# Pooling mixer begun with the attention mixer, a norm's spread four steps later, one weight split ahead of each norm

## The chip, the core and the metric

The kernel runs on one core of a Trainium2 chip. The metric is device time in microseconds of one execution. The core has four engines that compute, each with its own instruction stream, run in order: TensorE (PE) multiplies, VectorE (DVE), ScalarE (ACT) and GpSimd (POOL) do the elementwise work. SyncE (SP) issues the transfers from memory. Engines wait for each other by semaphores alone.

## The reference

Two transformer blocks over 256 tokens of width 1024, all in float32. What the change touches lies in the first block:

```python
def rmsnorm(x, w):
    return x * rsqrt(mean(x * x, -1) + EPS) * w

def pool_mixer(u, w_pool, scale):          # u: 256 tokens, 4 groups of 128 channels
    # trailing mean over 2, 4, 8, 16 tokens (one window a group) minus u itself,
    # then one 128x128 product a group, times scale
    p = stack([(c - lag) / cnt - u_g for each group])
    return einsum('btgc,gcd->btgd', p, w_pool).reshape(B, T, 512) * scale

def first_block(x, ...):
    proj = rmsnorm(x, norm_mix_pre) @ w_in
    gq, gk, gv, gg1, gr, pu, mq, mk, mv, gates = split(proj)
    ya = gla_mixer(gq, gk, gv, gg1, gr, ...) @ w_branch_a
    yb = pool_mixer(pu, pool_w, pool_scale) @ w_branch_b
    yc = moba_mixer(mq, mk, mv) @ w_branch_c       # here plain causal attention, 8 heads
    gs = sigmoid(gates)
    mixed = gs[0] * ya + gs[1] * yb + gs[2] * yc
    x = x + rmsnorm(mixed @ w_out, norm_mix_post)
    f = (silu(h @ w_gate) * (h @ w_up)) @ w_down   # h = rmsnorm(x, norm_ffn_pre)
    return x + rmsnorm(f, norm_ffn_post)
```

The second block has a feed-forward part, two attention mixers, a cross attention to a second input `mem`, and another feed-forward part. Keys and values of that memory are `rmsnorm(mem, mem_kv_norm) @ mem_w_kv`; their four products (`mkv0` to `mkv3`) are computed early, in the first block's time.

## The kernel before

**Units.** All weights lie in one flat array, cut into 360 units of 128x1024 numbers (512 KB) or less. SP fetches a unit into one of four buffers `raw`. ACT rounds it to an upper part `whi` (L1279), DVE subtracts to get the lower part `wlo` (L1627); together this is "the split of unit u". PE then multiplies three times: upper by upper, lower by upper, upper by lower (L806 to L808 where the weights are stationary or stream 512 columns, L814 to L817 where features stream 256). A unit is 12 matmuls of 512 columns or 24 of 256. The split of u needs the slot of u-4, so it waits until PE has multiplied u-4, and SP fetches u+4 once DVE has split u.

**The order.** One function, `order`, writes a list of steps, and every engine walks through this same list and issues its own share of each step. The order of each engine's instructions is fixed by it. The steps are: `split u`, `unit u`, `end name` (a finished product is taken out of PSUM), `do name`, and `step name`, one slice of a task that runs beside the products. `spawn` starts a task, `tick` gives each running task one step after each unit, in the order in which the tasks were spawned. A unit's splits stand `AHEAD = 2` units before it. Engines drift apart as far as the semaphores let them.

**The tasks the change touches.** `pool` has five steps. POOL adds the shifted sequences (L2263 to L2273, then the means at the margin, L2278), DVE forms mean minus input (L1879, tile `m_pp`) in step 2, PE multiplies with the group weights (L923) in step 5, ACT scales and rounds the result into `m_br_hi` (L1290 and L1291), DVE into `m_br_lo` (L1638), both in step 5. It is spawned after product `pu` (units 13 to 16), so its steps follow units 17 to 21 and run beside the task `gla` (25 steps, after units 9 to 33), whose masked copies out of PSUM are L1852 on DVE and whose score matmuls are L881 on PE. `moba` (15 steps) is spawned when `gla` is over, after product `gt1`, so its steps follow units 37 to 51: scores (L984) in step 4, row maxima (L1901) and their negation (L1907) on DVE, the exponential (L1403) on ACT in step 5, the transposes of its result (L961) on PE in step 6.

`memory` (12 steps, after units 53 to 64) loads, transposes and squares the second input; its root of the mean square is computed by POOL and DVE, and in the last step `across(4)` spreads it over the partitions: DVE writes two diagonals (L1672), PE multiplies them with ones (L848), DVE copies the result out (L1675). It is used first at the end of `mkv0`.

**Around each norm.** Products `wo0` and `wo1` (units 65 to 72, woven) and `f0dn0`, `f0dn1` (units up to 142) each end in `out_rms`: ACT squares (L1300), DVE scales (L1737). Then `sum_of` forms the root (L1743, POOL's power L2231, L1650 to L1656) and adds to x (L1750, four instructions). PE multiplies two units of the memory's keys in that time (73 and 74, and 143 and 144), then transposes half of the new x (L834), multiplies unit 75 (or 145), transposes the other half, and goes on.

PSUM has eight banks in two rings of four: big ones for the products of weights, small ones for all else. A small bank is taken again four takes later, and its next writer waits until the last reader is through.

Of the kernel before, what the change touches and what calls it, by code (L numbers as in the profile page):

```python
# [23 lines left out]
AHEAD = 2  # L24
# [261 lines left out]
for _n in range(11):  # L286
    for _name, _of in (("f0", "n1"), ("f1", "n2"), ("f2", "n6")):
        PRODUCTS[f"{_name}gu{_n}"] = ("b", _of)
NORMS = ("norm_mix_pre", "norm_ffn_pre", "ffn1_norm_2", "mix_norm_2", "mem_kv_norm_2", "mem_q_norm_2", "ffn2_norm_2")

STEPS = {"gla": 25, "pool": 5, "moba": 15, "fox": 13, "cmp": 9, "sel": 8, "win": 8, "mixed_first": 1, "mixed_second": 1, "yc": 1, "onsa": 1, "ofox": 1, "rel": 8, "memory": 12, "w1": 17,
         "gf_tokens": 2, "y_first": 1, "y_second": 1, **{f"mem{h}": 4 for h in range(4)}, "end_first": 2}
# [13 lines left out]
def order(chunks, n_units):  # L306
# [9 lines left out]
    def tick():  # L316
        for name in list(left):
            yield "step", name, 0, 0
            left[name] -= 1
            if not left[name]:  # L320
                del left[name]
                for n in THEN.get(name, ()):
                    spawn(n)
# [6 lines left out]
    def spawn(name):  # L330
        left[name] = STEPS[name]

    def do(name):
        yield "do", name, 0, 0

    def product(name, mid={}, end_first=False):
        for j, u in enumerate(chunks[name]):
            yield from split_to(u + AHEAD)
            if j in mid:
                yield from mid[j]()  # L340
            yield "unit", name, j, u
            if end_first and u == chunks[name][-1]:
                yield "end", name, 0, 0
            yield from tick()
        if not end_first:
            yield "end", name, 0, 0
# [11 lines left out]

    def woven(halves, mid={}, then={}):

        n = len(chunks[halves[0]]) // 2
        for i, (name, j) in enumerate((name, j) for first in (0, n) for name in halves for j in range(first, first + n)):
            u = chunks[name][j]
            yield from split_to(u + AHEAD)
            if i in mid:
                yield from mid[i]()
            yield "unit", name, j, u
            yield from tick()
            if j == 2 * n - 1:
                yield "end", name, 0, 0  # L370
                if name in then:
                    spawn(then[name])
# [10 lines left out]
    spawn("gla")  # L383
    for name in ("gr", "pu"):
        yield from product(name)
    spawn("pool")
    for name in ("mq", "mk", "mv"):
        yield from product(name)
    moba = False
    for n in range(6):  # L390
        yield from product(f"gt{n}")
        if not moba and "gla" not in left:
            spawn("moba")
            moba = True
    yield from drain()
    if not moba:
        spawn("moba")
        yield from drain()
    spawn("memory")
    for n in range(2):  # L400
        for i in range(3):
            yield from product(f"br{i}{n}")
        spawn(("mixed_first", "mixed_second")[n])
    yield from woven(("wo0", "wo1"))
    yield from drain()
# [5 lines left out]
    yield from product("f0dn0", {10: drain})  # L411
    yield from product("f0dn1")
    yield from do("sum1")
# [51 lines left out]
def build(nc, io):  # L465
    with ExitStack() as ctx:
# [248 lines left out]
        def gaps(i):  # L715
            return 2 if i == 5 else 3

# [553 lines left out]
        def scalar(q):  # L1271
# [228 lines left out]
            def memory():  # L1500
                for _ in range(6):
                    yield
                for n in range(2):
                    half(4, n)
                    squares(4, n)
                    yield
                for _ in range(3):
                    yield
# [792 lines left out]
        def sync(q):  # L2301
# [70 lines left out]
            def memory():  # L2372
                q.wait_ge(*ps.out("moba", "values", 1))
                load("mem", memx[:, :, :], io["mem_2"].rearrange("a (k p) d -> p (a k) d", p=128))
                for _ in range(11):
                    yield
# [111 lines left out]
```

## Time and profile before

| | |
|---|---|
| median of 3 runs | 1180.5 us (1178.74 to 1180.65) |
| the profiled execution | 1182.92 us, its span 1180.8 us |
| PE busy | 1136.7 us, 96% |
| DVE busy | 707.1 us, 60% |
| ACT busy | 562.4 us, 48% |
| POOL busy | 22.1 us, 2% |
| granted PE clock, mean | 0.986 of full |
| read from memory | 204.74 MB, 178 GB/s over the span |

All times in this document that have a place ("at 87.79") are microseconds from the span's start in the profiled execution. The profiled execution has 2.1 us around its span. A row of a timeline gives the start, the duration, the engine and the source line, then the tile that is written and those that are read, and in brackets how long the engine had been idle and what ended that. Neighbouring instructions of one kind are merged into one row, with their number behind the x. What PE is doing can be read only roughly from its busy share, since matmuls overlap; where its next start is late, it stood still.

### The profile page before, as it was taken

Reading aid. Unit: us, or ns where it says so; the run is one execution under the profiler, and the core shown is the slowest. Engines: PE = TensorE matmul, PEld = TensorE weight load, DVE = VectorE, ACT = ScalarE, POOL = GpSimd, SP = SyncE. Lnnn points to the kernel's source line nnn. Section 1 sums busy time; section 2 is a strip of 40 time slices with the busy share of each in tenths; the row PEclk is TensorE's granted clock in tenths of the full one; section 3 lists DMA queues with packets and bytes.
Section 4 is the critical chain, followed back from the end, with each engine's and each line's share of the span. In section 5 each row is a group of like instructions: output and inputs, shape, how many; then the busy total and the mean of one; then the engine's idle time right before and its main releaser. Section 6 shows DMA issues by size and latency. Waiting matters only on the chain.

```text
span 1180.8 us, 18370 instructions
## 1 busy us (share of the span) xinstructions
PE 1136.7 (96%) x7638; PEld 1021.9 (87%) x7638; DVE 707.1 (60%) x1069; ACT 562.4 (48%) x844; POOL 22.1 (2%) x43
## 2 busy tenths in 40 slices
PE   6989999999999999999999998999999999999996
PEld 6878878879999988899998897687888898999985
DVE  4676544867666646566665553355657556666653
ACT  5534556545444444544544436145654545544442
POOL 0030000000000000000000000000000000000000
PEclk9999999999999999999999998999999999999998
DMA  7544453554665764576656587222336335556561
GB/s 261 179 133 136 160 212 125 199 174 156 207 191 191 229 195 159 179 265 198 194 185 205 193 278 262 72 90 90 124 126 249 128 109 186 188 190 202 190 208 65
DMA packets 62653, 209.08 MB, mean 177 GB/s; under 512 B 7307, under 2 KB 14523, under 8 KB 61804
## 3 DMA queue, kind: packets, MB, share of 16 engines
q1 hardware_dynamic: 61148, 206.07, 52.9%
q10 hardware_dynamic: 1424, 1.85, 0.4%
q8 instruction: 60, 0.98, 0.3%
q14 instruction: 21, 0.17, 0.0%
HBM read 204.74 MB, written 5.26 MB: 178 GB/s over the span
## 4 chain that ended last, share of the span: by engine, by line
PE 85%; DVE 7%; ACT 3%; DMA 2%; issue 2%; POOL 1%; ACTq 0%; DVEq 0%; POOLq 0%
PE ps L814 13%; PE ps L806 12%; PE ps L817 12%; PE ps L816 12%; PE ps L808 12%; PE ps L807 12%; DMA raw<-in_wflat 2%; DVE wlo_b L1627 2%; PE ps L1059 1%; PE ps L834 1%; PE ps L1011 1%; PE ps L973 1%; ACT m_Pb L1403 1%; DVE wlo L1627 1%; PE ps L1046 1%
## 5 line engine op out<-in xcount | busy, mean ns | idle before, releaser
L814 PE MATMUL ps<-hT_hi,whi_b 128*128 128x256 f32 x1392 | 389.0, 279 | 5.2 <-DVE wlo_b L1627 5.2
L816 PE MATMUL ps<-hT_hi,wlo_b 128*128 128x256 f32 x1392 | 385.9, 277 | 0.0
L817 PE MATMUL ps<-hT_lo,whi_b 128*128 128x256 f32 x1392 | 385.6, 277 | 0.0
L1627 DVE TENSOR_TENSOR wlo_b<-raw,whi_b 128x1024 fp32r<-128x1024 f32 x184 | 219.1, 1212 | 124.2 <-ACT whi_b L1279 124.0
L1627 DVE TENSOR_TENSOR wlo<-raw,whi 128x1024 fp32r<-128x1024 f32 x176 | 212.3, 1222 | 117.3 <-ACT whi L1279 116.4
L814 PEld LDWEIGHTS ps<-hT_hi,whi_b 128*128 128x128 f32 x1392 | 262.8, 189 | 7.7 <-issue 5.6
L816 PEld LDWEIGHTS ps<-hT_hi,wlo_b 128*128 128x128 f32 x1392 | 262.9, 189 | 0.4
L817 PEld LDWEIGHTS ps<-hT_lo,whi_b 128*128 128x128 f32 x1392 | 262.7, 189 | 0.0
L1279 ACT ACTIVATE whi<-raw 128x1024 fp32r<-128x1024 f32 x176 | 181.6, 1057 | 112.9 <-PE ps L808 86.7
L1279 ACT ACTIVATE whi_b<-raw 128x1024 fp32r<-128x1024 f32 x184 | 184.1, 1042 | 32.7 <-PE ps L808 13.6
L806 PE MATMUL ps<-whi,hT_hi 128*128 128x512 f32 (+1 forms) x272 | 110.0, 404 | 0.0
L807 PE MATMUL ps<-wlo,hT_hi 128*128 128x512 f32 (+1 forms) x272 | 106.5, 392 | 0.0
L808 PE MATMUL ps<-whi,hT_lo 128*128 128x512 f32 (+1 forms) x272 | 106.5, 392 | 0.0
L806 PE MATMUL ps<-whi,f_hid_hi 128*128 128x512 f32 x264 | 102.8, 390 | 0.0
L807 PE MATMUL ps<-wlo,f_hid_hi 128*128 128x512 f32 x264 | 102.7, 389 | 0.0
L808 PE MATMUL ps<-whi,f_hid_lo 128*128 128x512 f32 x264 | 102.7, 389 | 0.0
L1345 ACT ACTIVATE f_sg<-f_sg 128x512 f32<-128x512 f32 x33 | 20.9, 633 | 125.0 <-DVE f_sg L1769 125.0
L806 PEld LDWEIGHTS ps<-whi,hT_hi 128*128 128x128 f32 x272 | 53.0, 195 | 13.1 <-issue 1.8
L808 PEld LDWEIGHTS ps<-whi,hT_lo 128*128 128x128 f32 x272 | 52.6, 193 | 10.8
L807 PEld LDWEIGHTS ps<-wlo,hT_hi 128*128 128x128 f32 x272 | 52.8, 194 | 9.2
L808 PEld LDWEIGHTS ps<-whi,f_hid_lo 128*128 128x128 f32 x264 | 49.6, 188 | 10.3
L806 PEld LDWEIGHTS ps<-whi,f_hid_hi 128*128 128x128 f32 x264 | 49.6, 188 | 10.2
(313 smaller groups left out, 1283.1 us busy)
## 6 DMA issues: line engine op xcount, KB each, us to landing
raw<-in_wflat SPq DMA_DIRECT2D x358, 512.0 KB, 4.1
wide<-scratch SPq DMA_DIRECT2D x1, 2048.0 KB, 10.8
m_w<-in_cmp_k_w SPq DMA_DIRECT2D x4, 512.0 KB, 9.4
m_w<-in_cmp_v_w SPq DMA_DIRECT2D x4, 512.0 KB, 8.9
m_alibi<-in_c_alibi SPq DMA_DIRECT2D x1, 1536.0 KB, 7.4
x<-in_x SPq DMA_DIRECT2D x2, 512.0 KB, 4.7
m_memx<-in_mem SPq DMA_DIRECT2D x1, 1024.0 KB, 5.9
kept_ck<-m_ckT SPq DMA_DIRECT2D x1, 1024.0 KB, 7.9
```

Source lines behind the costliest of these rows:

```text
L806: e.matmul(o, xh, hi[:, k, :], start=first and k == 0, stop=False)
L807: e.matmul(o, xh, lo[:, k, :], start=False, stop=False)
L808: r = e.matmul(o, xl, hi[:, k, :], start=False, stop=last and k == kt - 1)
L814: e.matmul(o, hi[:, k, c], xs.h(k0 + k), start=first and k == 0 and f % 2 == 0, stop=False, skip_group_check=True)
L816: e.matmul(o, lo[:, k, c], xs.h(k0 + k), start=False, stop=False, skip_group_check=True)
L817: r = e.matmul(o, hi[:, k, c], xs.l(k0 + k), start=False, stop=last and k == kt - 1, skip_group_check=True)
L834: r = e.transpose(s[:, 256 * i + 128 * t:256 * i + 128 * t + 128], src(t)[:, 128 * (f + i):128 * (f + i) + 128], ident)
L973: r = e.matmul(s[:, 64 * h:64 * h + 64], PT[:, h * (qb + 1) + k, :], value(h, k), start=k == 0, stop=k == qb)
L1011: r = e.matmul(s[:, 64 * h:64 * h + 64], PTs[qb][:, h * (qb + 1) + k, :], value(h, k), start=k == 0, stop=k == qb)
L1279: e.activation(slot(whi, u)[:, 0:k * n], raw[u % NRAW][:, 0:k * n], ACT.Copy).then_inc(*w_hi.did(u))
L1345: e.activation(b, b, ACT.Silu).then_inc(*silu.did(i, c))
L1627: e.tensor_tensor(slot(wlo, u)[:, 0:k * n], r, h.bitcast(F32), ALU.subtract).then_inc(*w_lo.did(u))
```

## The change

Three things are altered, all in the list that `order` writes and in the numbers of steps.

- `pool` is spawned together with `moba`, just ahead of it, after `gt1`, and no longer after `pu`. Its five steps now follow units 37 to 41, and on every engine each stands ahead of moba's step after the same unit.
- `gaps(4)` is 7, no longer 3: the last step of `memory` with `across(4)` follows unit 68 (the second of `wo1`), no longer unit 64. The numbers of empty steps on ACT and SP follow suit.
- `woven` and `product` take an argument `ahead`. For `wo0`/`wo1` and for `f0dn1` it is 3: behind the last unit, and ahead of the `end` step, one more split is written, that of unit 75 and of unit 145. (Units 73, 74, 143 and 144 are split there already.)

```diff
-"memory": 12,
+"memory": 16,
@@ product, woven @@
+            if u == chunks[name][-1]:
+                yield from split_to(u + ahead)
@@ order @@
-    for name in ("gr", "pu"):
-        yield from product(name)
-    spawn("pool")
-    for name in ("mq", "mk", "mv"):
+    for name in ("gr", "pu", "mq", "mk", "mv"):
         yield from product(name)
     moba = False
     for n in range(6):
         yield from product(f"gt{n}")
         if not moba and "gla" not in left:
+            spawn("pool")
             spawn("moba")
             moba = True
     yield from drain()
-    if not moba:
-        spawn("moba")
-        yield from drain()
     spawn("memory")
...
-    yield from woven(("wo0", "wo1"))
+    yield from woven(("wo0", "wo1"), ahead=AHEAD + 1)
...
-    yield from product("f0dn1")
+    yield from product("f0dn1", ahead=AHEAD + 1)
...
         def gaps(i):
-            return 2 if i == 5 else 3
+            return {4: 7, 5: 2}.get(i, 3)
```

The changed kernel's line numbers are one lower than those before, from `order` on. In the rows that follow, `wlo_b_67`, `wlo_68` and so on are the buffers of the lower part, one of them to a unit.

First place, DVE beside the early part of `gla`. Before:

```order
L1627 TENSOR_TENSOR wlo_b_65<-raw_52,whi_b_57 128x1024
L1852 COPY_PREDICATED m_acc<-m_msk,ps 128x2x128 x4
L1879 SCALAR_TENSOR_TENSOR m_pp<-m_t_102,m_pu 128x256
...
L1627 TENSOR_TENSOR wlo_b_67<-raw_53,whi_b_59 128x1024
L1852 COPY_PREDICATED m_acc<-m_msk,ps 128x2x128 x4
L1627 TENSOR_TENSOR wlo_b_69<-raw_54,whi_b_61 128x1024
```

In the changed kernel, the same place:

```order
L1626 TENSOR_TENSOR wlo_b_65<-raw_52,whi_b_57 128x1024
L1851 COPY_PREDICATED m_acc<-m_msk,ps 128x2x128 x4
L1626 TENSOR_TENSOR wlo_b_67<-raw_53,whi_b_59 128x1024
L1851 COPY_PREDICATED m_acc<-m_msk,ps 128x2x128 x4
L1626 TENSOR_TENSOR wlo_b_69<-raw_54,whi_b_61 128x1024
```

The four instructions that write `m_pp` are gone from between the splits of units 20 and 21; on PE the four products L923 are likewise gone from behind unit 21.

Second place, ACT at the first exponential of `moba` (`whi_62` is unit 43's upper part, `m_Pb` holds the scores). Before:

```order
L1322 ACTIVATE m_gates<-ps,stat 128x512 x2
L1279 ACTIVATE whi_62<-raw_55 128x1024
L1403 ACT_TABLE_LOAD
L1403 ACTIVATE m_Pb,sm<-m_Pb,sm 128x128 x8
L1279 ACTIVATE whi_56<-raw_52 128x1024
```

In the changed kernel:

```order
L1321 ACTIVATE m_gates<-ps,stat 128x512 x2
L1278 ACTIVATE whi_62<-raw_55 128x1024
L1289 ACTIVATE m_br_hi<-ps,cols 128x256
L1290 ACTIVATE m_br_hi<-ps,cols 128x256
L1289 ACTIVATE m_br_hi<-ps,cols 128x256
L1290 ACTIVATE m_br_hi<-ps,cols 128x256
L1402 ACT_TABLE_LOAD
L1402 ACTIVATE m_Pb,sm<-m_Pb,sm 128x128 x8
```

The pooled result's four instructions, which wait for PE's L923 behind unit 41, now stand between unit 43's upper part and the exponential; on DVE the four of `m_br_lo` stand ahead of L1907 in the same way.

Third place, DVE at the end of the branch products (`diag` and `rT` are of `across(4)`). Before:

```order
L1627 TENSOR_TENSOR wlo_66<-raw_53,whi_58 128x1024
L1627 TENSOR_TENSOR wlo_68<-raw_54,whi_60 128x1024
L1672 TENSOR_SCALAR diag<-cst,stat 128x128 x2
L1675 COPY rT_81<-ps 128x256
L1729 TENSOR_TENSOR m_mtmp<-ps,m_gates 128x512
```

In the changed kernel:

```order
L1626 TENSOR_TENSOR wlo_66<-raw_53,whi_58 128x1024
L1626 TENSOR_TENSOR wlo_68<-raw_54,whi_60 128x1024
L1728 TENSOR_TENSOR m_mtmp<-ps,m_gates 128x512
L1730 TENSOR_TENSOR m_mixed<-m_mixed,m_mtmp 128x512
```

The splits of units 65 and 66 are now followed at once by the mixing; the diagonals stand four splits further on.

## Rows read from the trace of the kernel before

**Rows 1.** The page, the chain of waits that ended last, by engine.

```profile
PE 85%; DVE 7%; ACT 3%; DMA 2%; issue 2%; POOL 1%; ACTq 0%; DVEq 0%; POOLq 0%
```

**Rows 2.** Timeline of PE, 79 to 91 us (columns as told above).

```profile
80.75 0.36 PE L814 MATMUL ps<-hT_hi,whi_b 128*128 128x256 f32 x1 [1.24 <-DVE wlo_b L1627]
...
87.79 2.88 PE L923 MATMUL ps<-m_pp,m_wpl 128*128 128x256 f32 x8 [2.72 <-DVE m_acc L1852]
90.11 0.78 PE L814 MATMUL ps<-hT_hi,whi_b 128*128 128x256 f32 x1
```

**Rows 3.** Timeline of DVE, 60 to 92 us.

```profile
70.12 2.35 DVE L1627 TENSOR_TENSOR wlo_b<-raw,whi_b 128x1024 fp32r<-128x1024 f32 x2
...
77.95 1.50 DVE L1879 SCALAR_TENSOR_TENSOR m_pp<-m_t,m_pu 128x256 f32<-128x256 f32 x4 [4.11 <-POOL m_t L2273]
```

**Rows 4.** Timeline of POOL, 60 to 92 us.

```profile
70.64 3.69 POOL L2266 TENSOR_TENSOR m_t<-m_pu 128x1084 f32<-128x1084 f32 x1
74.41 1.53 POOL L2268 TENSOR_TENSOR m_t<-m_t 128x807 f32<-128x807 f32 x1
```

**Rows 5.** Busy time by stretch: PE, PEld, DVE, ACT, POOL; then clock, DMA.

```profile
88.80:92.10 3.30, 3.30 (x13) 2.94 (x12) 1.39 (x4) 2.23 (x5) 0.00 (x0) 0.50 0.17 70
239.00:242.20 3.20, 3.20 (x9) 2.49 (x8) 3.13 (x6) 0.00 (x0) 0.00 (x0) 0.50 0.54 189
462.00:467.00 5.00, 3.46 (x29) 3.05 (x28) 5.00 (x7) 2.67 (x6) 0.00 (x0) 1.00 0.00 1
```

**Rows 6.** Timeline of DVE, 446 to 454 us, where PE sets the pace.

```profile
448.17 1.23 DVE L1627 TENSOR_TENSOR wlo<-raw,whi 128x1024 fp32r<-128x1024 f32 x1 [1.49 <-ACT whi L1279]
450.89 1.23 DVE L1627 TENSOR_TENSOR wlo_b<-raw,whi_b 128x1024 fp32r<-128x1024 f32 x1 [1.50 <-ACT whi_b L1279]
```

**Rows 7.** Timelines of POOL and of DVE, 118 to 150 us.

```profile
125.73 1.01 POOL L2231 TENSOR_TENSOR sm<-sm,expo 128x4 f32<-128x4 f32 x1
...
129.27 1.22 DVE L1627 TENSOR_TENSOR wlo<-raw,whi 128x1024 fp32r<-128x1024 f32 x1
...
143.72 3.50 DVE L1627 TENSOR_TENSOR wlo<-raw,whi 128x1024 fp32r<-128x1024 f32 x3 [5.31 <-ACT whi L1279]
```

**Rows 8.** Timeline of ACT: the pooled result, the exponential, another table load.

```profile
89.01 0.47 ACT L1290 ACTIVATE m_br_hi<-ps,cols 128x256 fp32r<-128x256 f32 x1 [13.36 <-PE ps L923]
...
156.61 0.40 ACT L1403 ACTIVATE m_Pb<-m_Pb,sm 128x128 f32<-128x128 f32 x1 [0.74 <-DVE sm L1907]
...
183.82 1.28 ACT L1322 ACT_TABLE_LOAD   x1
185.12 1.27 ACT L1322 ACTIVATE m_gates<-ps,stat 128x512 f32<-128x512 f32 x2
```

**Rows 9.** Timeline of PE, 155 to 160 us.

```profile
155.97 0.39 PE L808 MATMUL ps<-whi,hT_lo 128*128 128x512 f32 x1
...
159.86 0.33 PE L961 MATMUL ps<-cst,m_Pb 128*128 128x128 f32 x1 [0.78 <-ACT m_Pb L1403]
```

**Rows 10.** Timelines of PE and of DVE, 235 to 244 us.

```profile
238.12 0.71 PE L848 MATMUL ps<-diag,ones 128*128 128x128 f32 x4 [2.30 <-DVE diag L1672]
...
243.01 1.03 PE L834 MATMUL ps<-cst,m_mixed 128*128 128x128 f32 x8
243.80 0.47 PE L806 MATMUL ps<-whi,hT_hi 128*128 128x512 f32 x1
...
235.32 2.35 DVE L1627 TENSOR_TENSOR wlo<-raw,whi 128x1024 fp32r<-128x1024 f32 x2
...
239.21 0.68 DVE L1729 TENSOR_TENSOR m_mtmp<-ps,m_gates 128x512 f32<-128x512 f32 x1
```

**Rows 11.** Timelines of PE at both norms, and of ACT at the first.

```profile
271.16 0.38 PE L814 MATMUL ps<-m_n_hi,whi_b 128*128 128x256 f32 x1 [1.35 <-DVE wlo_b L1627]
...
465.92 0.38 PE L814 MATMUL ps<-m_n_hi,whi_b 128*128 128x256 f32 x1 [1.31 <-DVE wlo_b L1627]
...
263.14 0.60 ACT L1300 ACTIVATE junk<-ps 128x512 f32<-128x512 f32 x1 [2.13 <-PE ps L808]
```

More of the change, by code:

```diff
@@ L289 @@
 NORMS = ("norm_mix_pre", "norm_ffn_pre", "ffn1_norm_2", "mix_norm_2", "mem_kv_norm_2", "mem_q_norm_2", "ffn2_norm_2")
-STEPS = {"gla": 25, "pool": 5, "moba": 15, "fox": 13, "cmp": 9, "sel": 8, "win": 8, "mixed_first": 1, "mixed_second": 1, "yc": 1, "onsa": 1, "ofox": 1, "rel": 8, "memory": 12, "w1": 17,
+STEPS = {"gla": 25, "pool": 5, "moba": 15, "fox": 13, "cmp": 9, "sel": 8, "win": 8, "mixed_first": 1, "mixed_second": 1, "yc": 1, "onsa": 1, "ofox": 1, "rel": 8, "memory": 16, "w1": 17,
          "gf_tokens": 2, "y_first": 1, "y_second": 1, **{f"mem{h}": 4 for h in range(4)}, "end_first": 2}
@@ L334, in do, with product @@
         yield "do", name, 0, 0
-    def product(name, mid={}, end_first=False):
+    def product(name, mid={}, end_first=False, ahead=0):
         for j, u in enumerate(chunks[name]):
@@ L357, in ffn, with woven @@
             spawn(f"turn{i}_{c}")
-    def woven(halves, mid={}, then={}):
+    def woven(halves, mid={}, then={}, ahead=0):
         n = len(chunks[halves[0]]) // 2
@@ L368, in woven @@
             yield from tick()
+            if u == chunks[halves[1]][-1]:
+                yield from split_to(u + ahead)
             if j == 2 * n - 1:
@@ L1506, in memory @@
                     yield
-                for _ in range(3):
+                for _ in range(gaps(4)):
                     yield
@@ L2374, in memory @@
                 load("mem", memx[:, :, :], io["mem_2"].rearrange("a (k p) d -> p (a k) d", p=128))
-                for _ in range(11):
+                for _ in range(15):
                     yield
```

## The prediction

> **What bounds the kernel now.** I read the chain of waits first. PE holds 85% of it, DVE 7%, ACT 3% [rows 1], so an edit is worth what it takes out of PE's standing still, and nothing else. Then I went through PE's timeline for late starts. They add up to some 30 us in the whole span; five of them stand where the change touches something. The rest of PE's time is units, one every 2.72 us: where PE alone sets the pace, DVE's splits start 450.89 - 448.17 = 2.72 us apart [rows 6].
>
> The first two are in the early part of `gla`. PE's unit 21 starts at 80.75 after 1.24 us idle, waiting for its lower part, and the pooling product L923 starts at 87.79 after 2.72 us idle, waiting for a small bank that DVE's masked copies free late [rows 2]. Both have one cause: at 77.95 DVE had stood 4.11 us for POOL's window sums [rows 3], with the split of unit 21 queued behind. The third is `across(4)`: 2.30 us idle before L848, waiting for DVE's diagonal [rows 10]. The last two are at the norms: 1.35 and 1.31 us before unit 75 and unit 145, waiting for a split that DVE does only after it has added to x [rows 11].
>
> The holes cost more than their length. After the one that ends at 87.79 the granted clock is 0.50, that is 1.2 instead of 2.4 GHz, from 88.8 to 92.1, and after the one that ends at 238.12 again from 239.0 to 242.2. After the hole of 1.31 us it stays 1.00 [rows 5].
>
> **The change part by part.** Places are given in the time of before, without the shift gained earlier.
>
> *Pooling leaves the early place.* DVE's four L1879 and the wait of 4.11 us go, so unit 21's split is done near 75.0 instead of 80.6. PE starts unit 21 when its score matmuls end: 1.2 us gained. Then nothing stands between the last score matmuls and unit 22: the hole of 2.7 us goes, and the product itself, which held PE from 87.79 to 90.11, 2.3 us [rows 2]. Of the half-clock stretch 90.11 to 92.1 is unit work, 2.0 us at half speed, so 1.0 us comes back; with the switching between kinds of matmul, 0.1 to 0.2 us, I take 1.2. Together 7.4 us. What is late next? Unit 22 would start near 83.8; DVE has split it by 78. The score matmuls after unit 25 come near 94.8; they need banks that the masked copies of the previous pair free near 84.6, and DVE's eight products before them are through near 90. Nothing else on SP or POOL is passed: SP's list is unchanged, and the two powers of POOL that pooling is moved past come forward. Bounds: at least the two waits' own 1.2 + 2.7 = 3.9, at most 7.7.
>
> *Pooling enters the late place.* POOL can begin once its second power is through, 125.73 + 1.0 = 126.7 [rows 7]. Its sums took from 70.64 to about 77.9, 7.3 us [rows 4, 3], so they end near 134. DVE wants them behind the split of unit 40, the second of the three at 143.72 [rows 7], so near 146: no wait, 12 us to spare. The 1.5 us of L1879 lie in DVE's slack (5.31 us idle ahead of that row).
>
> The product is another matter. PE does it after unit 41, whose last matmul starts at 155.97 [rows 9], so from 156.2. Eight passes over 256 columns, at the pace of the transposes (eight over 128 in 243.80 - 243.01 = 0.79 us [rows 10]), are 1.6 us; I take 1.7. ACT took up the pooled result 1.22 us after the product began (89.01 against 87.79 [rows 8, 2]), so now at 157.4. Four activations, 0.4 us apart, end at 159.0. Behind them in ACT's queue stands the table load for the exponential, 1.28 us [rows 8]; before, it lay in time in which ACT waited anyway. So the exponential starts at 160.3 instead of 156.61 [rows 8]: 3.7 us later. DVE's lower parts end near 159.9 and the negated maxima at 160.1, just hidden. PE's transposes L961 already waited for the exponential (0.78 us idle at 159.86 [rows 9]); they now start at 163.5. This term is -3.7 us, product included. Bounds: -1.7 (the product alone, everything else hidden) to -4.3 (the product as slow as before, 2.3 us).
>
> PE has only the product and unit 42 to fill the time: 156.2 + 1.7 + 2.7 = 160.6. It stands still for 2.9 us. Holes of this size in the same company were followed by the half clock twice [rows 2, 10, 5], so I expect a stretch of 3.4 us at half speed behind it, in unit work: -1.7 us. Bounds 0 to -1.8.
>
> By the Trainium skill, "ScalarE: Activation LUTs", section "What ACT_TABLE_LOAD costs", a switch costs a drain of about 1.38 us on top of the load. The trace does not show it: the load at 183.82 took 1.28 us and the next activation starts at 185.12 [rows 8]. With it, the term of the exponential would be -5.1 and the total 1.4 us smaller.
>
> *The spread four steps later.* Without the diagonals, PE goes from unit 64 (over at 235.7) to unit 65, which waits for DVE's split: the first of the two that start at 235.32 [rows 10], so to 236.5. Then unit 65 to 239.2, and the transposes of `mixed`, which need the four mixing instructions. DVE starts these at 237.6 instead of 239.21, at 0.66 us each (0.68 with overlap [rows 10]), so they end at 240.3. The transposes start there instead of at 243.01 [rows 10]: 2.7 us gained, in place of the 2.30 us hole two of 0.8 and 1.1 us. In it is 1.6 us for a half-clock stretch that falls away; if it stays, 1.1 is left. At its new place PE's L848 stands after unit 68, near 249; DVE's diagonal is written before that, near 247, and its user comes 25 us later. The copy that waits there for PE has the split of unit 71 behind it, done near 251.5 and needed at 255. Bounds +1.0 to +3.0.
>
> *One split ahead, twice.* ACT's part of unit 75 falls in the 2.13 us in which it waits for the last unit of `wo1` [rows 11], since it needs only unit 71. DVE's, 1.2 us, follows and ends 0.4 us before the squares release L1737. So nothing is pushed back, and the holes of 1.35 and 1.31 us at the two norms go: with the overlap of matmuls 1.45 each, 2.9. The next thing due, unit 76, is split within 1.2 us of x. Bounds 2.2 to 3.0.
>
> **The sum.** 7.4 - 3.7 - 1.7 + 2.7 + 2.9 = 7.6 us. Against the profiled execution's 1182.92 that gives 1175.3; it lay 2.4 above the median of the three runs, so for the median I say 1180.5 - 7.6 = 1172.9.
>
> **The rivals.**
>
> *No half clock at the exponential.* For it: the clock after the 1.31 us hole stayed full, so not every hole is followed by a slow stretch. Against it: 2.30 and 2.72 us idle both were. 1180.5 - 9.3 = 1171.2.
>
> *POOL and DVE hinder each other at the new place.* POOL's L2266 took 3.69 us for 1084 elements, 3.4 ns each, while DVE was in its two splits from 70.12; L2268, with DVE idle, took 1.53 us for 807, 1.9 ns each [rows 3, 4]. So POOL is slowed by DVE, and DVE was not slowed: 2.35 us for two splits is their usual length. At the new place POOL runs from 126.7 beside the splits of units 34 to 38, and if it were DVE that is held, for at most the 5.4 us that the four sums take alone, then PE's unit 34 at 133, whose split ended at 130.5 [rows 7], would be up to 2.9 us late. 1172.9 + 2.9 = 1175.8. The Trainium skill, "SBUF — State Buffer", section "SBUF: two separate sides", has one port pair for both engines, held by whichever starts first for its whole instruction; for POOL's lost time the trace agrees, for DVE's no row shows it.
>
> *The half clock also at the two small holes* of 0.8 and 1.1 us before the mixing: 1172.9 + 1.6 = 1174.5. Only the closeness of the two speaks for it.
>
> *The waits are handed on.* If DVE is the true bound at these places, each wait that goes is taken over by the next item in its queue, and every term lies at its lower bound: 3.9 - 4.3 - 1.7 + 1.0 + 2.2 = 1.1 us, so 1179.4, no measurable change. For it: DVE is busy for all of 462 to 467 [rows 5] and stands behind four of the five holes. Against it: the slack of several microseconds worked out above.
>
> *Slower: POOL late at the new place.* DVE waits in order at L1879 behind unit 40, with the splits of 41 and 42 behind it; each microsecond that POOL is later than 146 holds PE for one. POOL needs 7.3 us from 126.7, and at its slow rate of 3.4 ns an element throughout 9.2, ending at 136. It would decide from 146 on, and make the kernel slower only beyond 146 + 7.6 + 2.4, that is 156, four times as long; then 1183 or more.
>
> **How the numbers follow.** 0.50 for the forecast, 0.25 for no half clock at the exponential, 0.10 for the hindrance, 0.07 for the half clock at the small holes, 0.05 for no net gain, 0.03 for slower. Within 0.2% (2.4 us, about what can be told from no change) lies the fifth alone. So faster 0.92, same 0.05, slower 0.03. The range 1169.5 to 1176.5 takes in the first four with the runs' own spread of 1 us either side.
>
> **What would show it.** Right: no wait of DVE for POOL near 78; score matmuls of the second pair of heads about 7.5 us earlier; L848 with no idle time; units 75 and 145 straight behind the transposes; at L961 about 2.9 us idle for ACT, with the four L1290/L1291 and the table load just ahead of the exponential, and a clock of 0.50 behind it. Wrong: a new wait of PE between units 21 and 34, DVE waiting at L1879, or L1737 held by the early split.

## The result: 1175.5 us, half of the forecast gain

The changed kernel takes 1175.52 us, median of 20 runs (1170.95 to 1181.41), against 1180.51 for 20 runs of the kernel before. The ratio, run beside run, is 0.9968, with a 95% interval of 0.9953 to 0.9983: 3.8 us less, between 2.0 and 5.5. The medians lie 5.0 us apart, but the ratio compares runs taken side by side, and I go by it. The forecast was 7.6 us. Measured twice more, beside other runs of the kernel before, the ratio was 0.9965 and 0.9949.

The profiled execution lasted 1172.54 us with a span of 1170.4. Against the profiled one of before that is 10.4 us less, far more than the ratio, so the two spans can't be subtracted as they stand. I take the trace in two parts: up to the second norm, where most of the difference can be put down to places, and behind it, where single executions differ among themselves by 6 us (told below). "The lead" at a unit is how much earlier than in the kernel before DVE starts that unit's split. In the kernels of the experiments the line numbers are shifted by a few.

**Chain by engine** of the changed kernel, which answers to [rows 1]:

```profile
PE 86%; DVE 6%; ACT 3%; issue 2%; DMA 1%; POOL 0%; ACTq 0%; POOLq 0%; DVEq 0%
```

**The early place.** DVE beside `gla`, then the busy time by stretch (PE, PEld, DVE, ACT, POOL; clock, DMA):

```profile
75.72 1.45 DVE L1851 COPY_PREDICATED m_acc<-m_msk,ps 128x256 f32<-128x256 uint8 x4 [0.66 <-PE ps L880]
77.05 1.22 DVE L1626 TENSOR_TENSOR wlo_b<-raw,whi_b 128x1024 fp32r<-128x1024 f32 x1
```

```profile
83.40:100.00 16.60, 16.60 (x138) 14.81 (x134) 12.64 (x24) 6.46 (x8) 0.00 (x0) 1.00 0.47 161
```

DVE's wait of 4.11 us for POOL [rows 3] is gone, and so are PE's two late starts [rows 2] and the clock of 0.50 [rows 5]: PE is busy for all of 16.6 us at full clock. DVE's split of unit 24 starts at 85.12; before, it did at 92.53. That is a lead of 7.4 us, the forecast to the tenth.

**The late place.** POOL and DVE side by side from 119 us on, then what PE made of it:

```profile
119.66 2.05 POOL L2265 TENSOR_TENSOR m_t<-m_pu 128x1084 f32<-128x1084 f32 x1
121.79 1.54 POOL L2267 TENSOR_TENSOR m_t<-m_t 128x807 f32<-128x807 f32 x1
...
125.71 2.60 POOL L2277 TENSOR_TENSOR sm<-m_t,cst 128x16 f32<-128x16 f32 x4
```

```profile
119.78 1.95 DVE L1649 TENSOR_TENSOR sm<-sm 128x4 f32<-128x4 f32 x1
121.77 0.16 DVE L1651 TENSOR_TENSOR sm<-sm 128x4 f32<-128x4 f32 x1
121.96 1.39 DVE L1653 TENSOR_SCALAR sm<-sm 128x4 f32<-128x4 f32 x1
...
124.96 2.91 DVE L1626 TENSOR_TENSOR wlo<-raw,whi 128x1024 fp32r<-128x1024 f32 x2
```

```profile
126.76 0.50 PE L805 MATMUL ps<-whi,hT_hi 128*128 128x512 f32 x1 [0.57 <-DVE wlo L1626]
```

Two operations of four columns each, L1649 and L1653, take 1.95 and 1.39 us; their neighbour L1651 takes 0.16. The first ends at 121.73, with POOL's L2265 (121.71); the second at 123.35, with L2267 (123.33). L1651 began at 121.77, between the two, 0.02 us ahead of POOL's L2267, and was not held. DVE's two operations thus lasted until POOL's instruction was over each time. PE is late for it at 126.76, at unit 34, and the lead over the kernel before falls from 7.4 to 6.2 us by unit 39.

Then the exponential, ACT and PE, answering to [rows 8, 9]:

```profile
151.05 0.47 ACT L1289 ACTIVATE m_br_hi<-ps,cols 128x256 fp32r<-128x256 f32 x1 [2.69 <-PE ps L922]
...
152.77 1.28 ACT L1402 ACT_TABLE_LOAD   x1
154.07 0.40 ACT L1402 ACTIVATE m_Pb<-m_Pb,sm 128x128 f32<-128x128 f32 x1
```

```profile
154.22 0.39 PE L807 MATMUL ps<-whi,hT_lo 128*128 128x512 f32 x1
157.30 1.09 PE L960 MATMUL ps<-cst,m_Pb 128*128 128x128 f32 x8 [2.70 <-ACT m_Pb L1402]
```

This is the path of the forecast, link by link, and its price too: from unit 39 to unit 45 the lead falls by 3.7 us, to 2.6. The clock does not do what I forecast. It stays full behind this hole and falls 33 us later, behind a smaller one:

```profile
157.30:161.00 3.70, 3.70 (x21) 3.20 (x22) 2.96 (x4) 3.68 (x5) 0.00 (x0) 1.00 0.17 18
...
190.20:196.80 6.60, 6.60 (x21) 5.54 (x21) 2.96 (x3) 0.00 (x0) 0.00 (x0) 0.50 0.39 141
```

```profile
187.38 4.57 PE L972 MATMUL ps<-m_mv,m_PT 128*128 128x64 f32 x32 [1.01 <-DVE m_PT L1914]
```

The slow stretch cost 3.2 us (from unit 47's split to unit 55's 37.3 us instead of 34.1), and the lead is gone: DVE's split of unit 55 is 0.6 us later than before. The kernel before has the same hole of 1 us there, and no slow stretch behind it (PE, 188 to 192 us, then the busy time by stretch):

```profile
189.94 2.30 PE L973 MATMUL ps<-m_mv,m_PT 128*128 128x64 f32 x19 [1.01 <-DVE m_PT L1915]
...
190.00:194.00 4.00, 4.00 (x34) 3.96 (x35) 1.19 (x2) 1.15 (x2) 0.00 (x0) 1.00 0.66 247
194.00:198.00 4.00, 4.00 (x19) 3.25 (x19) 2.69 (x3) 0.00 (x0) 0.00 (x0) 1.00 0.35 110
```

**The spread**, PE, answering to [rows 10]:

```profile
237.33 0.47 PE L805 MATMUL ps<-whi,hT_hi 128*128 128x512 f32 x1 [0.86 <-DVE wlo L1626]
...
241.12 1.06 PE L833 MATMUL ps<-cst,m_mixed 128*128 128x128 f32 x8 [0.78 <-DVE m_mixed L1730]
...
250.23 0.60 PE L847 MATMUL ps<-diag,ones 128*128 128x128 f32 x4
250.59 0.48 PE L805 MATMUL ps<-whi,m_br_hi 128*128 128x512 f32 x1
```

The two small holes of the forecast are there, and no diagonals between them: 2.5 us gained by unit 68. At their new place, behind unit 68, the diagonals take 0.5 us again, so 2.0 are left at unit 73. **The norms**, answering to [rows 11]: PE starts unit 75 and unit 145 straight behind the transposes of x, and waits 0.2 us ahead of these. The first:

```profile
267.42 1.06 PE L833 MATMUL ps<-cst,x 128*128 128x128 f32 x8 [0.20 <-DVE x L1749]
268.24 0.36 PE L813 MATMUL ps<-m_n_hi,whi_b 128*128 128x256 f32 x1
```

1.6 us gained at each. So the sum up to unit 149 is 7.4 - 1.2 - 3.7 - 3.2 + 2.0 + 3.2 = 4.5 us. The trace has the same 4.5: DVE's split of that unit, in the kernel before and in the changed one.

```profile
474.92 1.23 DVE L1627 TENSOR_TENSOR wlo<-raw,whi 128x1024 fp32r<-128x1024 f32 x1 [1.02 <-ACT whi L1279]
```

```profile
470.39 1.23 DVE L1626 TENSOR_TENSOR wlo<-raw,whi 128x1024 fp32r<-128x1024 f32 x1 [0.89 <-ACT whi L1278]
```

The lead stays at 4.5 us up to unit 216, at 650 us. Behind it the two traces part further, to 10 us at the end, with no instruction in another order. Compared with the kernel before, the changed one has 3.4 us less of half clock near 720, none near 860, and shorter waits for the weights' DMA between 680 and 740 (ACT waits 4.7 us for them there, before 14.3). The next experiment shows that the same kernel can lack this gain.

### The profile page after: what moved, and what is told of

The parts are those of the page before. It is cut to its first block, busy times and chain, and to the rows that moved or that the text cites. A ratio compares the mean times of both kernels' runs of the same rounds, so it can differ in the third digit from the quotient of the medians.

```text
span 1170.4 us, 18373 instructions
## 1 busy us (share of the span) xinstructions
PE 1133.3 (97%) x7638; PEld 1019.1 (87%) x7638; DVE 709.5 (61%) x1069; ACT 563.1 (48%) x844; POOL 22.9 (2%) x43
## 4 chain that ended last, share of the span: by engine, by line
PE 86%; DVE 6%; ACT 3%; issue 2%; DMA 1%; POOL 0%; ACTq 0%; POOLq 0%; DVEq 0%
PE ps L813 13%; PE ps L816 13%; PE ps L815 13%; PE ps L805 12%; PE ps L806 12%; PE ps L807 12%; PE ps L833 1%; PE ps L1058 1%; DVE wlo L1626 1%; PE ps L972 1%; PE ps L1010 1%; DVE wlo_b L1626 1%; DMA raw<-in_wflat 1%; ACT m_Pb L1402 1%; PE ps L880 1%
## 5 line engine op out<-in xcount | busy, mean ns | idle before, releaser
L806 PEld LDWEIGHTS ps<-wlo,f_hid_hi 128*128 128x128 f32 x264 | 49.6, 188 | 10.2
```

The source lines that it names most:

```text
L806: e.matmul(o, xh, lo[:, k, :], start=False, stop=False)
```

## The experiments

The experiments were run in four groups, each with its own runs of the kernel before: the first four (after_again and the three parts) have a median of 1178.99 us for it, the second four (late_product, sums_wait, both_late, filled) 1179.55, the third four (filled_second, late_filled, both_filled, both_no_spread) 1178.47, the last three 1180.28. All gains below are from the ratio.

### Again, and the three parts alone

*after_again*: the changed kernel, unaltered.

> The whole change once more, for a second trace and for runs with their granted clock beside runs of the kernel before on the same chip. Theory 1 (a smaller gain on PE's path, and time at the half clock that differs from run to run): ratio 0.996 to 0.998; a run's time rises by 0.3 to 0.5 us per us at the half clock; at equal half-clock time this kernel is 5 to 7 us ahead; the half-clock stretches lie elsewhere than in the first trace, while DVE's slow L1649 and L1653 at 119.8 and 122.0 are there again. Rival (the 7.6 us of the prediction are real, and the first series was unlucky): ratio 0.9925 to 0.9945.

1174.63 us, ratio 0.9965 (0.9949 to 0.9981). Its profile agrees with the first within 0.1 us up to unit 149, and ends 6 us later:

```profile
470.33 1.23 DVE L1626 TENSOR_TENSOR wlo<-raw,whi 128x1024 fp32r<-128x1024 f32 x1 [0.89 <-ACT whi L1278]
```

What it has more is mostly half clock, in the second part of the kernel (near 719, 790, 801 and 859). The weights' DMA has a part as well: between 680 and 740 ACT waits 11.8 us for it instead of 4.7, and at unit 232, ahead of the first difference in clock, this execution is already 0.5 us behind. The runs, too, go with the clock: among the 20 of the changed kernel, the two fastest (1170.95 and 1171.04) have a mean clock of 0.991, and those above 1179 have 0.981 to 0.983. Over all runs the mean clock is 0.9873 for the changed kernel (44 runs) and 0.9872 for the kernel before (89). So no difference in the total of half clock can be seen; the change altered where some of it lies. At this equal mean clock the three ratios of the changed kernel (mean 0.9961) make 4.6 us, somewhat under the 5 to 7 that I had expected.

*pool_only*, *spread_only* and *ahead_only*: one part of the change each, on the kernel before.

```diff
# pool_only: order
-    spawn("pool")                    (after pu)
+            spawn("pool")            (with moba)
# spread_only: gaps, memory's steps
-            return 2 if i == 5 else 3
+            return {4: 7, 5: 2}.get(i, 3)
# ahead_only
+    yield from woven(("wo0", "wo1"), ahead=AHEAD + 1)
+    yield from product("f0dn1", ahead=AHEAD + 1)
```

> Only the pooling mixer is moved. Theory 1: early place +7.4, late place -3.7, POOL and DVE in each other's way behind gla -1.2, so 2.5 us ahead at equal half-clock time; the hole of 2.9 us at L961 brings half-clock stretches in part of the runs, so 0.5 to 2.5 us in the mean (ratio 0.998 to 1.000). Rival (no hindrance, the half clock as before): 3.7 us, ratio 0.997.

1179.43 us, ratio 1.0008 (0.9992 to 1.0023): nothing gained, 0.9 us at best. Its trace has the half clock twice, behind the exponential's hole as forecast, and near 190 as well:

```profile
158.50:161.70 3.20, 3.20 (x12) 2.91 (x13) 2.46 (x4) 2.96 (x4) 0.00 (x0) 0.50 0.09 14
192.60:199.20 6.60, 6.60 (x22) 5.63 (x22) 2.96 (x3) 0.00 (x0) 0.00 (x0) 0.50 0.39 133
```

> Only across(4) goes four steps on. Theory 1: the hole of 2.3 us before it becomes two of about 1 us; 1.1 us by the path, and 0 to 1.6 more where the half clock behind the old hole goes (ratio 0.9975 to 0.999). Rival (DVE is the bound there and hands its wait on): no change.

1178.27 us, ratio 0.9993 (0.9981 to 1.0005): 0.8 us, not told from none, nor from the 1.1 of the path alone. Its trace is 2.5 us ahead at unit 73, 0.5 of it from the start of the span; the runs don't bear out the 2.0.

> Only the splits of units 75 and 145 are put ahead of the norms. Theory 1: 2.9 us, ratio 0.9975, with no change in half-clock time. Rival (given back behind the norm, where ACT and DVE are due next): under 1 us.

1175.65 us, ratio 0.9967 (0.9954 to 0.9979): 3.9 us. The splits ahead alone bring what the whole change brings. The largest edit, worth 7.4 us at one place, is paid for at the other, in full as far as the runs can tell.

### What the late place costs

*late_product*: the product one step later on PE, ACT's and DVE's part two steps later.

```diff
-"pool": 5,
+"pool": 7,
@@ pool on PE: L922 after unit 42, ahead of L961 @@
-                for _ in range(4):
+                for _ in range(5):
@@ pool on ACT @@
-                for _ in range(4):
+                for _ in range(6):
```

> The changed kernel, with the pooling product one step later on PE: after unit 42, straight ahead of the transposes that wait for the exponential, so that ACT's four activations on it and the table load no longer stand ahead of the exponential. Theory A (the loss at the new place is the exponential being late, and the slow stretch near 190 follows from the hole of 2.86 us that PE has at 154): the exponential starts near 151.5 again, the hole is gone, PE loses there the product's 1.7 us less the 0.95 us that it stood idle before anyway, 0.8 in place of 3.7 us; and no half clock follows near 190, 3.3 us more. Together 6 us less than the changed kernel: near 1169. Rival B (the half clock near 190 has nothing to do with the hole at 154): 2.9 us only, near 1171.7, with a clock of 0.50 still there near 187 to 194. Rival C (the wait is handed on to the transposes' evictions and the values): no gain, 1174.6.

1170.99 us, ratio 0.9926 (0.9899 to 0.9954). By the ratios that is 4.1 us less than the changed kernel. ACT loads the table beside PE's units again, and PE has no hole:

```profile
148.20 1.28 ACT L1403 ACT_TABLE_LOAD   x1
150.53 0.40 ACT L1403 ACTIVATE m_Pb<-m_Pb,sm 128x128 f32<-128x128 f32 x1 [1.05 <-DVE sm L1906]
```

```profile
152.53 1.89 PE L922 MATMUL ps<-m_pp,m_wpl 128*128 128x256 f32 x8
154.26 1.04 PE L961 MATMUL ps<-cst,m_Pb 128*128 128x128 f32 x8
```

The lead at unit 47 is 5.7 us. Of the exponential's 3.7 us, 0.7 is left: the rest is shown to be the pooled result's work ahead of it. The edit moves ACT's four activations and DVE's four lower parts alike. That ACT's are what held the exponential is read from the first trace: the table load and the exponential follow them without a pause, while DVE was through 0.3 us earlier (L1906 at 153.58, for 0.16 us):

```profile
151.92 1.74 DVE L1637 SCALAR_TENSOR_TENSOR m_br_lo<-ps,cols,m_br_hi 128x256 fp32r<-128x256 f32 x4 [1.33 <-ACT m_br_hi L1290]
153.58 0.16 DVE L1906 TENSOR_SCALAR sm<-sm 128x8 f32<-128x8 f32 x1
```

But in late_product the half clock near 190 stays, without the hole that was to explain it. Theory A was right on the first half and wrong on the second; its rival B had forecast just this:

```profile
186.80:193.40 6.60, 6.60 (x23) 5.63 (x23) 2.96 (x3) 0.00 (x0) 0.00 (x0) 0.50 0.36 130
```

*sums_wait*: one wait more on POOL, ahead of the window sums.

```diff
                 q.wait_ge(*pu_z.at())
+                q.wait_ge(*ps.out("x", "gla", 1))
```

> The changed kernel, with POOL's window sums started only when gla's result has left its bank, so that they don't run while DVE does its small operations on the gates and the splits of units 33 and 34. Theory (the 1.2 us that PE lost between units 24 and 39, and the DVE operations of 1.95 and 1.39 us in place of 0.16 and 0.17 us, come from POOL and DVE running at once): those two go back to 0.2 us, the split pair at 125 back to 2.35 us, the gaps of PE at 125.9 go, and the shift against the kernel before stays near -7.4 us up to the exponential: 1.2 us less, 1173.4; POOL still ends before DVE wants its sums. Rival (the POOL sums lengthen DVE's work wherever they run, and only the place changes): the splits beside them at the new time take more than 2.5 us a pair and the gain is 0: 1174.6.

1173.35 us, ratio 0.9955 (0.9937 to 0.9973). DVE's gate operations are short again, and PE's gap at 126 is gone; the lead at unit 39 is 7.6 us instead of 6.2:

```profile
119.55 0.15 DVE L1649 TENSOR_TENSOR sm<-sm 128x4 f32<-128x4 f32 x1
...
119.94 0.17 DVE L1653 TENSOR_SCALAR sm<-sm 128x4 f32<-128x4 f32 x1
...
128.49 3.02 DVE L1626 TENSOR_TENSOR wlo<-raw,whi 128x1024 fp32r<-128x1024 f32 x1
```

```profile
127.66 2.76 POOL L2266 TENSOR_TENSOR m_t<-m_pu 128x1084 f32<-128x1084 f32 x1
```

The runs alone can't tell this from no gain (the ratio is 0.7 us under the changed kernel's mean, inside the intervals); the trace does. Theory and rival were both half right. The hindrance did not vanish, it moved: a split now takes 3.02 us instead of 1.2, to 131.5, one microsecond beyond POOL's 130.4. But PE doesn't stand behind that split. Its trace has the half clock behind the exponential's hole (156.3 on) and none near 190.

*both_late*: the two edits together.

> The two edits together: product after unit 42, window sums after gla's result. If both theories hold they add up, since the places are 25 us apart: 6 + 1.2 us less than the changed kernel, near 1167.5. With the half clock near 190 still there: 1170.5. This is the version meant to beat both kernels; if it comes out within 1 us of the changed kernel, both terms were wrong.

1166.84 us, ratio 0.9897 (0.9873 to 0.9921): 12.1 us less than before. Repeated as *both_again*:

> both_late once more, on whatever chip this is, to see whether it stays ahead of the changed kernel: 0.990 of the time of before, 5 to 7 us less than the changed kernel. Theory (the stretch near 187 depends on the moment): it may be there this time. Rival (the two edits remove it for good): it is not.

1170.10 us, ratio 0.9910 (0.9884 to 0.9936), beside the changed kernel at 0.9949. Both times it beats both kernels, the changed one by 7.5 us (0.9897 against 0.9961, the mean of its three ratios) and by 4.6, a little under the 5 to 7 expected. Neither trace has a half clock between 80 and 700.

*both_no_spread*: `both_late` with `gaps(4)` back at 3.

> both_late with memory root's across back at three steps apart, as in the kernel before. Theory (the spread is worth what the holes of PE say, 2.30 us idle against 1.02 + 0.95, with the switch to the diagonals, 1.1 us, and the half clock that it removed in the trace comes back elsewhere): 1 us slower than both_late, 1167.9. Rival (the half clock behind the hole of 2.30 us counts in full, as in the forecast): 2.7 us slower, 1169.5, with a clock of 0.50 behind the hole before L847.

1168.91 us, ratio 0.9923 (0.9903 to 0.9943): 2.3 us slower than the mean of both_late's two ratios, with intervals that hold both theories. The trace decides for 1.1: from unit 24 to unit 149 the lead over the kernel before grows by 3.3 us here, and by 4.4 in both traces of both_late. And there is no half clock behind the hole of 2.3 us, though the kernel before had one [rows 5, 10]. From unit 65's split to unit 68's the kernel before takes 10.4 us, this one 9.5, and both_late 7.9: the half clock behind the diagonals cost 0.9 us, the way of the instructions 1.6.

```profile
231.25 0.71 PE L847 MATMUL ps<-diag,ones 128*128 128x128 f32 x4 [2.28 <-DVE diag L1672]
```

```profile
231.30:234.70 3.40, 3.40 (x16) 2.57 (x16) 2.63 (x5) 0.00 (x0) 0.00 (x0) 1.00 0.80 281
```

### Which hole the half clock follows

Four kernels fill a hole of PE with matmuls whose result is overwritten, and a fifth has such matmuls where there is no hole. In the rows each such matmul counts twice. *filled* is the changed kernel with the hole at the exponential filled:

```diff
-                    q.wait_ge(*expd.at(name, qb))
...
+                        if b == 0:
+                            if name == "moba" and qb == 0:
+                                for _ in range(12):
+                                    e.matmul(s[:, 0:128], ones[:, :], ident, start=True, stop=True)
+                            q.wait_ge(*expd.at(name, qb))
```

> The changed kernel with 12 matmuls of 128 columns that nobody reads put into the hole of 2.86 us ahead of the first transposes L960; at 0.21 us each they fill 2.6 us of it and delay nothing. The output is unchanged. Theory A (the slow stretch of 6.8 us near 190 follows from the hole at 154, since it stands in all three traces that have this hole and in none of the three that don't): no half clock between 150 and 200, and 3.3 us less than the changed kernel, 1171.3. Rival B (the stretch follows from the hole of 1.17 us right ahead of it and from where that falls in time, which is 2 to 3 us earlier than in the kernel before): the same stretch, 1174.6. Rival C (busy or not, the exponential is what sets it): the same as B.

1172.17 us, ratio 0.9939 (0.992 to 0.9958). The added matmuls stand where PE waited, and its trace has no half clock from 150 to 200; from unit 24 to unit 149 it gains 3.2 us on the changed kernel's:

```profile
155.73 2.84 PE L961 MATMUL ps<-cst,ones 128*128 128x128 f32 x24
158.59 1.09 PE L964 MATMUL ps<-cst,m_Pb 128*128 128x128 f32 x8
```

By itself that speaks for theory A. But late_product has the stretch without this hole, and the trace of filled keeps the small hole of 1.01 us, which ends at 188.67, with no stretch behind it. So the small hole was filled next, in *filled_second* (the changed kernel) and *late_filled* (late_product), with 4 such matmuls ahead of the values' waits of the second block.

```diff
+                        if name == "moba" and qb == 1 and b == 0:
+                            for _ in range(4):
+                                e.matmul(s[:, 0:128], ones[:, :], ident, start=True, stop=True)
                         q.wait_ge(*ps.out(name, "turned", qb, b))
```

> The changed kernel with 4 matmuls of 128 columns that nobody reads put into the hole of 1.17 us ahead of the values' matmuls L972 of the second block; at 0.21 us each they fill 0.85 us of it. The output is unchanged. Theory A (the slow stretch of 6.8 us near 190 is set off by this small hole, since the late_product kernel has the stretch without the hole at 154): no half clock between 180 and 200, 3.3 us less than the changed kernel in the trace there. Rival B (it is set by the hole of 2.86 us at 154, and the late_product trace is an exception): the stretch stays. In the time, over many runs, A gives up to 3.3 us less than the changed kernel, 1171.3, B nothing, 1174.6.

1172.74 us, ratio 0.995 (0.9932 to 0.9967). The slow stretch near 190 is gone; this trace has one behind the exponential's hole instead:

```profile
158.60:161.80 3.20, 3.20 (x12) 2.91 (x13) 2.46 (x4) 2.94 (x4) 0.00 (x0) 0.50 0.05 6
186.00:190.00 4.00, 4.00 (x25) 3.44 (x23) 2.34 (x4) 4.00 (x7) 0.00 (x0) 1.00 0.45 141
190.00:196.00 6.00, 5.89 (x44) 5.40 (x43) 3.19 (x5) 1.43 (x2) 0.00 (x0) 1.00 0.51 171
```

> late_product with the same 4 matmuls in the hole of 1.17 us. late_product has no hole at 154 and yet the clock at 0.50 from 186.7 on. Theory A: the stretch goes, and the trace stands 3.3 us ahead of late_product's from there on; time near 1168. Rival B (neither hole sets it, it is the matmuls of 64 columns themselves, L972, that let the clock fall): it stays, 1171.

1168.39 us, ratio 0.9918 (0.9899 to 0.9936). Gone here as well: no half clock from 80 to 700, and from unit 24 to unit 149 the lead grows by 3.2 us, against 0.1 in late_product. As theory A had it; the ratios differ by only 0.9 us, within their intervals.

*both_filled* is `both_late` with the same 4 matmuls.

> both_late with the 4 matmuls in the hole of 1.17 us. both_late has no half clock near 187 already, so by either theory nothing is gained or lost in its trace: 1166.8 within 1 us. If it is more than 1 us slower, the added matmuls delay the values' matmuls.

1168.35 us, ratio 0.9921 (0.9903 to 0.994), with no half clock near 187 in the trace, as in both_late. It is 2.8 and 1.3 us above both_late's two ratios, within the intervals; by what I had written that would mean that the added matmuls delay the values, but the trace shows no such delay (the lead is 5.7 us at unit 47 and at unit 55).

*both_moved*: `both_late` with 10 such matmuls ahead of L961, where PE has no hole.

> both_late with 10 matmuls of 128 columns that nobody reads ahead of the first transposes L961, where PE has no hole: they make everything behind them 2.1 us later and change nothing else, the hole of 1.17 us ahead of L973 keeps its length. The output is unchanged. Theory (whether the half clock follows that hole is decided by the moment at which the hole falls, not by its length): the trace may show a stretch of 0.50 behind L973 at this place although both_late had none; the time is that of both_late plus 2.1 us, and up to 3.3 us more where the stretch comes: 1168.9 to 1172.2. Rival (the hole at 154 is needed for it): no stretch, 1168.9.

1171.63 us, ratio 0.9929 (0.9903 to 0.9955), 3.0 us above both_late's mean, which decides neither for theory nor for rival. The trace:

```profile
154.34 2.39 PE L962 MATMUL ps<-cst,ones 128*128 128x128 f32 x20
...
186.56 1.63 PE L977 MATMUL ps<-m_mv,m_PT 128*128 128x64 f32 x13 [0.98 <-DVE m_PT L1918]
```

```profile
189.10:195.60 6.50, 6.50 (x22) 5.53 (x22) 2.96 (x3) 0.00 (x0) 0.00 (x0) 0.50 0.36 123
```

No hole at the exponential, the small hole of 0.98 us as in both_late, 3.2 us later than in its first trace and 1.9 later than in its second, and the stretch of 6.8 us is there, which neither trace of both_late has. So the large hole isn't needed for it, as late_product had shown already. And *after_third*, the changed kernel once more:

> The changed kernel a third time, beside both_late on the same chip: 0.9966 of the time of before. Theory (moment): the stretch near 190 may be missing in this trace. Rival (it belongs to the hole of 2.86 us at 154): the stretch is there again.

1174.26 us, ratio 0.9949 (0.9925 to 0.9973). The same instructions in the same order as in the first trace, and this time both stretches:

```profile
157.20:160.40 3.20, 3.20 (x12) 2.91 (x13) 2.46 (x4) 2.94 (x4) 0.00 (x0) 0.50 0.06 10
187.50:191.00 3.50, 2.52 (x22) 2.26 (x21) 2.26 (x3) 2.48 (x3) 0.00 (x0) 1.00 0.54 167
191.40:198.00 6.60, 6.60 (x22) 5.63 (x22) 2.96 (x3) 0.00 (x0) 0.00 (x0) 0.50 0.36 134
```

The table counts all 17 traces, that of before among them:

| hole of PE (idle) | traces with it | half clock behind it | in traces where it is filled or gone |
|---|---|---|---|
| pooling product, early (2.7) | 3 | 3 | 0 of 14 |
| exponential (2.7) | 6 | 4 | 0 of 11 (0.8 us or none) |
| values of the second block (1.0) | 14 | 6 | 0 of 3 |
| diagonals (2.3) | 4 | 2 | 0 of 13 (two of 0.8) |

From 20 to 700 us a stretch came only behind one of these holes, and the same hole of the same kernel brought it in one trace and not in the next. Other holes brought none: two of 0.9 us near 64 and 72 in all 17 traces, the six of 1.3 to 1.35 us at the norms (two each in before, pool_only and spread_only), the two of 0.8 us that the spread leaves. So the length of the hole alone doesn't decide: 1.3 us was followed by no stretch in these six cases, 1.0 us was in 6 of 14.

What is shown: from 20 to 700 us the half clock came behind holes alone, a hole doesn't suffice, and the exponential's is not needed for the one near 190. That filling the small hole prevents the stretch is likely but not shown, since 8 of the 14 traces with the hole have none either. What makes the difference stays open. The moment, counted from the start of the span, doesn't sort the traces: PE's next matmul starts at 188.77 in after_third, with a stretch, and at 188.67 in filled, without; at 184.28 in late_product, with, and at 184.69 in both_again, without.

## Why the prediction was half right

*Early place, +7.4*: right in the sum; how much of it was half clock no run tells apart, since all three kernels with that hole have the stretch. *The exponential, -3.7*: right, and late_product shows the cause. *Splits ahead, +2.9*: right, 3.2 in the trace, 3.9 in the runs of ahead_only.

**The step that failed is the account of the half clock.** It entered single stretches of one trace as fixed terms: -1.7 behind the exponential, and gains for two that fall away, 1.6 of them at the spread. The hole ahead of the second block's values it put at nothing. "Holes of this size in the same company were followed by the half clock twice, so I expect a stretch of 3.4 us" generalised from two places of one trace. Where the stretch behind the exponential came, it cost 1.5 to 1.6 us, so its size was right; but it came in four traces of six, and in one of the changed kernel's three. The small hole, which both kernels have and which my sum did not contain, cost 3.2 us in all three traces of the changed kernel. Of the five holes I looked at none was this one, since the diff doesn't touch it. Over many runs the mean clock is the same with and without the change, 0.9873 and 0.9872. Two stretches of 3.4 us less and one more would have raised it by about 0.0014 (half of 3.4 us in 1175); worked out from the spread of the runs, the difference is known to about 0.0011.

**A second step failed by being left out of the sum:** *the hindrance of POOL and DVE*. It had 0.10 as a rival, "if it were DVE that is held". It was DVE, for 1.2 us on PE, under the 2.9 that I had as the bound, and PE's late unit 34 is the wait "between units 21 and 34" that I had named as a sign of being wrong. sums_wait shows the cause. The row I argued from, DVE's two splits of 2.35 us beside POOL [rows 3, 4], showed only the case in which DVE was first. I also had the wrong partner: POOL ran beside gla's short operations on the gates, not only beside the splits. The Trainium skill, "SBUF — State Buffer", section "SBUF: two separate sides", says that between a GpSimd instruction and a DVE instruction with two SBUF inputs or in a 2-port mode, whoever starts first keeps the shared ports for its whole instruction. The trace agrees: L1649 began 0.12 us behind POOL's L2265 and ended 0.02 behind it. I had set the rule beside the trace and then let one row, which could not contradict it, count against it.

*The spread, +2.7*: 2.0 in the trace, 0.8 in the runs. Two sizes were off. Half a microsecond is PE's own time for the diagonals, 250.59 - 250.23 = 0.36 and a slower first matmul behind them: I took it out of the old place and forgot it at the new one. And the half clock that falls away there cost 0.9 us and not 1.6, and is no property of the kernel: both_no_spread and pool_only have the hole and not the stretch. Without it the spread is worth 1.6 - 0.5 = 1.1 us.

By the trace, 7.6 - 1.2 - 1.5 - 0.7 + 0.3 = 4.5 us: the hindrance, the half clock at 3.2 instead of 1.7, the spread, the splits ahead. The runs' 3.8 (2.0 to 5.5) agree. That the first trace comes so near the runs is partly luck: after_third, the same kernel, has both stretches and a lead of only 3.1 us at unit 149. Of the other rivals, "no half clock at the exponential" is what two of the changed kernel's three traces show there; at the two small holes of the spread none came in any trace; "the waits are handed on" and "POOL late" did not happen: DVE's L1878 didn't wait.

```profile
139.79 1.42 DVE L1878 SCALAR_TENSOR_TENSOR m_pp<-m_t,m_pu 128x256 f32<-128x256 f32 x4
```

## What to carry to other kernels

When work is moved into slack, look not only at the engine that does it but at what stands behind its results in every other queue: with four short activations ahead of a table load the pooled result cost 3.7 us; with its product one step later and the activations two, 0.7. Before moving work onto POOL, list DVE's short operations at the new place that PE waits for; beside splits with slack the same hindrance cost PE nothing in sums_wait. Count half clock as a chance behind a hole, those outside the diff too, and never as a term from one trace. Compare kernels by the trace place by place, and by the total only up to where several executions of one kernel still agree: two of the changed kernel did for 650 us, the third only up to the exponential.

## What I had not expected of the hardware

- Idle time of 1.0 us on PE ahead of matmuls of 64 columns was followed by 6.8 us of half clock, a cost of 3.2 us, in 6 of 14 traces. Behind the exponential's 2.7 us it was 3.4 us, a cost of 1.5 to 1.6, 4 times in 6. Behind the six holes of 1.3 to 1.35 us at the norms there was none.
- Two executions of one kernel, equal within 0.1 us for 650 us, ended 6 us apart, most of it by half clock, some by the weights' DMA.
- A DVE operation of four columns took 1.95 us beside one of POOL, against 0.15 without it. POOL is slowed as well: L2265 over 1084 elements took 2.05 us here, 2.76 beside splits in sums_wait, and 3.69 in the kernel before [rows 4].
- With the load of 1.28 us ahead of it, the exponential at 154.07 followed within 0.02 us. The further drain of 1.38 us in the Trainium skill, "ScalarE: Activation LUTs", section "What ACT_TABLE_LOAD costs", is not seen in this case.
